# A two-layer decoder step on one core: the result sent in column groups by SP's queue, small transposes joined, decode rows of the first projection in quarters

## What is computed

```python
def block(h, p_l, pos, lw, nsa_fn, h0_re, h0_im, conv_prefix):
    z = rmsnorm(h, g_attn) @ w_in                  # queries, three pairs of K/V, branch gates, S5 input, two merge gates
    o_cmp, o_sel, o_win, rows = nsa_fn(q, kc, vc, ks, vs, kw, vw, ...)
    o = bg[..., 0:1] * o_cmp + bg[..., 1:2] * o_sel + bg[..., 2:3] * o_win
    a_out = o.reshape(B, T, Q_W) @ w_a             # mixer A
    y, hr, hi = ssm_scan(u, ...)                   # mixer B: a recurrence over the positions
    yg = gelu(y)
    b_out = (yg @ w_glu1) * sigmoid(yg @ w_glu2)
    h = h + (sigmoid(ga) * a_out + sigmoid(gb) * b_out) @ w_o
    gp, val = split(rmsnorm(h, g_ffn) @ w_up)
    ext = concatenate([conv_prefix, gp])           # two rows of state for each sequence
    conv = conv_b + sum(conv_w[j] * ext[:, j:j + T] for j in range(3))
    h = h + (gelu(conv) * val) @ w_down
    h = h + sigmoid(rmsnorm(h, g_ple) @ w_ple_gate) * (p_l @ w_ple)
    return h, rows, hr, hi, ext[:, T:]             # the last two rows of ext are an output too
```

## Time and profile before

| | us |
|---|---|
| median of 3 runs | 1161.51 (1161.04 to 1164.3) |
| profiled execution, its time | 1160.05 |
| its span, first to last instruction | 1158.2 |
| PE busy | 1113.9 |
| DVE, ACT, POOL busy | 474.6, 292.2, 157.8 |

### The profile page before, as it was taken

How to read it: one execution, slowest core, us unless ns; L and a number is a source line. 1 busy time by engine, 2 the same in 40 slices (tenths; PEclk the granted TensorE clock), 3 DMA queues, 4 the chain that set the end, 5 groups by cost and what they waited for, 6 DMA issues and landing times.

```text
span 1158.2 us, 16487 instructions
## 1 busy us (share of the span) xinstructions
PE 1113.9 (96%) x6314; PEld 918.5 (79%) x6314; DVE 474.6 (41%) x1197; ACT 292.2 (25%) x929; POOL 157.8 (14%) x276
## 2 busy tenths in 40 slices
PE   6999999999999999999999999999999999999995
PEld 4887776688888888888888878667888888888884
DVE  5889606623432222152435863472334222210031
ACT  4435424501111111210344462361112111110021
POOL 5544320003000000005003623000000000000000
PEclk9999999999999999999999999999999999999998
DMA  9653683146555553444655367222355555445431
GB/s 246 178 143 95 162 252 91 37 146 150 155 152 151 150 147 100 129 125 155 186 155 145 110 172 269 66 91 97 131 139 143 146 148 147 129 119 150 145 112 37
DMA packets 239423, 162.23 MB, mean 140 GB/s; under 512 B 25344, under 2 KB 233240, under 8 KB 239208
## 3 DMA queue, kind: packets, MB, share of 16 engines
q1 hardware_dynamic: 229858, 144.45, 43.6%
q0 software_dynamic: 4752, 14.58, 4.3%
q10 hardware_dynamic: 4736, 2.16, 0.7%
HBM read 157.94 MB, written 7.58 MB: 143 GB/s over the span
## 4 chain that ended last, share of the span: by engine, by line
PE 87%; DVE 7%; ACT 3%; issue 1%; DMA 0%; DVEq 0%; SPq 0%; POOL 0%; ACTq 0%; POOLq 0%
PE bank_act L695 40%; PE bank_dve L695 36%; DVE kT L1788 1%; PE bank_dve L997 1%; PE bank_act L880 1%; PE bank_act L1073 1%; PE bank_o L1087 1%; PE bank_o L1039 1%; ACT L1217 1%; PE bank_dve L826 1%; DVE Sf L1777 1%; DVE pcw L1795 0%; DVE vpast L1791 0%; DVE rstd L1749 0%; DVE Sf L1792 0%
## 5 line engine op out<-in xcount | busy, mean ns | idle before, releaser
L695 PE MATMUL bank_act<-xn,ring 128*128 128x264 f32 x1568 | 366.9, 391 | 6.2 <-DVE xn L1753 5.3
L695 PEld LDWEIGHTS bank_act<-xn,ring 128*128 128x128 f32 x1568 | 298.8, 192 | 64.4 <-issue 9.2
L695 PE MATMUL bank_dve<-R,ring 128*128 128x264 f32 x704 | 157.6, 386 | 0.0
L695 PE MATMUL bank_dve<-xn,ring 128*128 128x264 f32 x672 | 156.4, 386 | 0.0
L695 PEld LDWEIGHTS bank_dve<-R,ring 128*128 128x128 f32 x704 | 133.4, 190 | 22.6
L695 PEld LDWEIGHTS bank_dve<-xn,ring 128*128 128x128 f32 x672 | 127.7, 190 | 21.8
L1970 DVE TENSOR_SCALAR PT<-GX,PT 128x264 f32<-128x264 f32 x44 | 18.3, 417 | 200.6 <-ACT GX L1217 200.5
L1217 ACT ACTIVATE GX<-bank_act 128x264 f32<-128x264 f32 x44 | 17.2, 391 | 269.1 <-PE bank_act L695 269.1
L1217 ACT ACTIVATE xn<-hT 128x264 f32<-128x264 f32 x32 | 13.5, 423 | 202.4 <-DVE hT L1989 149.8
L643 POOL DMA_DIRECT2D out_dram<-kall x2 | 1.0, 520 | 454.4 <-ACT kall L1217 454.4
L1217 ACT ACTIVATE PT<-bank_act 128x10 f32<-128x10 f32 (+4 forms) x94 | 28.8, 307 | 129.7 <-PE bank_act L695 123.6
(11 more groups left out here) (372 smaller groups left out, 1371.4 us busy)
## 6 DMA issues: line engine op xcount, KB each, us to landing
ring<-in_w_up_dram SPq DMA_DIRECT2D x88, 512.0 KB, 5.1
ring<-in_w_in_dram SPq DMA_DIRECT2D x28, 1024.0 KB, 6.0
ring<-in_w_down_dram SPq DMA_DIRECT2D x32, 704.0 KB, 4.6
ring<-in_w_glu_dram SPq DMA_DIRECT2D x16, 512.0 KB, 4.5
ring<-in_w_o_dram SPq DMA_DIRECT2D x8, 1024.0 KB, 5.0
ring<-in_w_ple_gate_dram SPq DMA_DIRECT2D x8, 1024.0 KB, 5.1
PT<-in_cache_cmp_dram SPq DMA_DIRECT2D x64, 64.0 KB, 2.4
ring<-in_w_a_dram SPq DMA_DIRECT2D x8, 512.0 KB, 6.9
```

Of the source, the lines that this page charges most:

```text
L695: ins = pe.matmul(out, lhsT, rhs, start=(k == 0), stop=(k == nk - 1))
```

## The change

- The result: tiles 0 to 3 of `hT` are turned between the third and the fourth chunk of the last layer's gate product, and DVE copies them after its sixth tile. The epilogue turns tiles 4 and 5 (ACT copies), 6 and 7 (DVE copies) and the 8 decode rows (ACT copies). SP sends the prompt's rows in three DMAs of 512, 256 and 256 columns, each after the copy that it needs; ACT's queue sends the decode rows; POOL only waits.
- Compressed weights: `SP_` gets a pitch of 32, and 4 transposes of 128x128 turn all heads at once, ahead of the turn of the decode outputs; ACT copies one bank of 128x512 to `pcmp`. `head_out` reads 15 rows at partitions 0, 32, 64 or 96. So the prompt's compressed values are made on all four of these, by 8 products with 32 weight columns in place of 2 with 15 in the third bank, and ACT copies that bank in two instructions. DVE splits one product of 16 sums in two.
- Conv state: in by 4 transposes of 110x128, out by 2 of 128x110 in one bank. `conv_rows` takes 4 loads of 512-byte rows instead of 3, the output 9 DMAs instead of 2.
- Decode rows of the first projection: from a layer's second chunk on, four quarters at output rows 0, 32, 64 and 96, copied in four pieces.

```diff
+            y_rows = y_prompt.rearrange("b (t p) d -> p (b t) d", p=P)
+            for c0, c1, freed, count in ((0, 512, dve_freed, dve_jobs(DEPTH - 1, "result", 2)), (512, 768, act_freed, A_BASE[DEPTH] + 1),
+                                         (768, D, dve_freed, V_BASE[DEPTH] + 1)):
+                sp.wait_ge(freed, count)
+                sp.dma_start(y_rows[:, :, c0:c1], xrows[:, 0:2, c0:c1]).then_inc(y_out, 16)
...
+                    for s in range(NB):
+                        row = KF * ((s + 2) % 5)
+                        pool.dma_start(conv_s.rearrange("l s j (f x) -> (l s j f) x", x=P)[ds((L * NB + s) * 2 * KF + KF, KF), :],
+                                       gp_rows[row:row + KF, (s + 2) // 5, :]).then_inc(conv_out, 16)
...
-                pool.dma_start(y_prompt.rearrange("b (t p) d -> p (b t) d", p=P), xrows[:, 0:2, :]).then_inc(y_out, 16)
-                pool.dma_start(y_sample.rearrange("s a d -> s (a d)"), xrows[0:NB, 2, :]).then_inc(y_out, 16)
...
-                                for j in range(2):
-                                    last = pe.matmul(bank[64 * j:64 * j + NB, 0:n // 2], rows[k][:, SEQ:NT], w[:, k, n // 2 * j:n // 2 * (j + 1)],
+                                parts = 2 if jobs <= U_AT else 4
+                                for j in range(parts):
+                                    a, m = P // parts * j, n // parts
+                                    last = pe.matmul(bank[a:a + NB, 0:m], rows[k][:, SEQ:NT], w[:, k, m * j:m * j + m],
                                                      start=(k == 0), stop=(k == KD - 1))
...
-                    for i in range(3):
+                    for i in range(3 if j < 2 else 2):
...
+                    for i in range(4 if j == 2 else 0):
+                        for g in range(KV):
+                            c = NSEQ * KV * NCMP + (g * NSEQ + NB) * NCMP
+                            last = pe.matmul(bank[32 * i:32 * i + 32, 256 + HD * g:256 + HD * g + HD], Sf[:, c:c + 32], w2[:, 2, :],
                                              start=True, stop=True)
...
+                pe.wait_ge(c_prob, L + 1)
+                bank = act_bank()
+                for j in range(2):
+                    for t in range(2):
+                        at = 2 * P * t + P * j
+                        last = pe.transpose(bank[:, P * (2 * j + t):P * (2 * j + t + 1)], SPf[:, at:at + P], ident)
+                last.then_inc(act_ready, 1)
...
-                for f in range(KF):
-                    last = pe.transpose(bank[:, 20 * f:20 * f + 20], conv_rows[:, P * f:P * f + P], ident[0:20, 0:20])
+                for k in range(4):
+                    last = pe.transpose(bank[:, 5 * KF * k:5 * KF * (k + 1)], conv_rows[:, k, :], ident[0:5 * KF, 0:5 * KF])
...
-                for j in range(6):
-                    bank = act_bank()
-                    for f in range(4 * j, min(4 * j + 4, KF)):
-                        last = pe.transpose(bank[0:10, P * (f - 4 * j):P * (f - 4 * j) + P], gcol[:, f, :], ident)
-                    last.then_inc(act_ready, 1)
+                bank = act_bank()
+                for k in range(2):
+                    last = pe.transpose(bank[0:5 * KF, P * k:P * k + P], gcol[:, 5 * k:5 * k + 5, :].rearrange("p t f -> p (t f)"), ident)
+                last.then_inc(act_ready, 1)
...
+                    if i == 2 and L + 1 == DEPTH:
+                        pe.wait_ge(h_done, L * KD + KD + 4)
+                        for t in range(3):
+                            m = P if t < 2 else NB
+                            bank = dve_bank()
+                            for k in range(4):
+                                last = pe.transpose(bank[0:m, P * k:P * k + P], hT[:, k, P * t:P * t + m], ident)
+                            last.then_inc(dve_ready, 1)
...
-                        pieces = 1 if t < 2 else 2
+                        pieces = 1 if t < 2 else 2 if jobs <= U_AT else 4
```

More of the change, by code:

```diff
@@ L156, in probs_turned @@
 def probs_turned(L, u):
[L158 removed]
+    return act_jobs(L, "p_probs", u + 1 + sum(v <= u for v in GATES_IN_HEADS))
 def weight_chunks(L):
@@ L1446, in _ @@
                     fn(hg[:, v, :], bank[:, 0:2 * NSEQ * NCMP], ACT.Gelu_apprx_tanh, bias=pe_col[:, v:v + 1]).then_inc(act_freed, 1)
-                for j in range(3):
+                for j in range(2):
                     fn(vcmp[:, 3 * j:3 * j + 3, :], take(base)[0:NCMP, 0:3 * KVW].rearrange("p (s d) -> p s d", s=3)).then_inc(act_freed, 1)
+                bank = take(base)
+                fn(vcmp[:, 6:NB, :], bank[0:NCMP, 0:2 * KVW].rearrange("p (s d) -> p s d", s=2))
+                fn(vprompt, bank[:, 2 * KVW:3 * KVW]).then_inc(act_freed, 1)
                 act_.wait_ge(s_max, L + 1)
@@ L1529, in _ @@
                 gelu(KF - 1)
-                for j in range(6):
-                    w = P * min(4, KF - 4 * j)
-                    fn(gp_rows[:, 4 * P * j:4 * P * j + w], take(base)[0:10, 0:w]).then_inc(act_freed, 1)
+                fn(gp_rows, take(base)[0:5 * KF, 0:2 * P].rearrange("p (k x) -> p k x", k=2)).then_inc(act_freed, 1)
                 for o in range(KD):
@@ L1556, in _ @@
             n[0] = 0
-            for t in range(3):
-                m = P if t < 2 else NB
-                last = fn(xrows[0:m, t, 0:512], take(A_BASE[DEPTH])[0:m, :]).then_inc(act_freed, 1)
+            fn(xrows[:, 0:2, 512:768], take(A_BASE[DEPTH])[:].rearrange("p (t d) -> p t d", t=2)).then_inc(act_freed, 1)
+            fn(xrows[0:NB, 2, 512:D], take(A_BASE[DEPTH])[0:NB, :]).then_inc(act_freed, 1)
+            act_.wait_ge(act_freed, A_BASE[DEPTH] + 2)
+            act_.wait_ge(dve_freed, dve_jobs(DEPTH - 1, "result", 3))
+            act_.dma_start(y_sample.rearrange("s a d -> s (a d)"), xrows[0:NB, 2, :]).then_inc(y_out, 16)
         @block.vector
@@ L2010, in _ @@
                     stt(hT[:, o, :], cv[:, o % 2, :], 0.5, hT[:, o, :], MUL, ADD).then_inc(h_done, 1)
+                    if o == 5 and L + 1 == DEPTH:
+                        for t in range(3):
+                            m = P if t < 2 else NB
+                            dve.tensor_copy(xrows[0:m, t, 0:512], take(base)[0:m, :]).then_inc(dve_freed, 1)
                     if L + 1 < DEPTH:
@@ L2018, in _ @@
             n[0] = 0
-            for t in range(3):
-                m = P if t < 2 else NB
-                dve.tensor_copy(xrows[0:m, t, 512:D], take(V_BASE[DEPTH])[0:m, :]).then_inc(dve_freed, 1)
+            dve.tensor_copy(xrows[:, 0:2, 768:D], take(V_BASE[DEPTH])[:].rearrange("p (t d) -> p t d", t=2)).then_inc(dve_freed, 1)
 def constants():
```

106 lines of the change are left out of this document (52 added, 54 removed).

## The result

The changed kernel takes 1146.84 us (median of 4, 1144.20 to 1150.21); the kernel before, run again beside it, 1162.12 (1161.04 to 1164.3). The ratio is 0.9871, with a 95% interval of 0.9841 to 0.9901. The forecast was 1150, range 1143 to 1154. The profiled execution took 1144.20, its span 1142.3: 15.9 us less than the span before, where the sum of the steps had said 11.6.

What follows compares the result with a forecast made beforehand. PE was taken as the bound, busy 1113.9 of 1158.2 us. Terms -2.8 + 1.2 - 3.1 + 0 - 4.5 - 2.4 = -11.6 from the profiled 1160.05 gave 1148.45, 1150 for the median; range 1143 to 1154.

Steps and rivals of the forecast that it cites:

- E: Conv state out, between gate tiles and down product: 22 transposes per layer become 2, nothing absorbs the gain; -4.5 us.
- C: Compressed weights in the attention: 16 small transposes per layer leave, 4 wide ones hide in a wait; -3.1 us.
- D: Conv state in, ahead of the product with w_o: 22 transposes become 4, but PE only waits longer; 0.
- A: First projection's decode rows in quarters, eight blocks: 6.6 us off PE's list, mostly absorbed by waits; -2.8 us.
- B: Compressed values, third bank: a second ACT copy and more small PE products, 0.6 per layer; +1.2 us.
- F: Result at the kernel's end: earlier transposes, shorter last copies, smaller last DMA; -2.4 us.
- rival 2: Program's end: the unnamed 6.7 us after the last landing is POOL closing its queue, some 6 can go; 1144, chance 0.20.
- rival 5: Decode blocks: the four quarters run one after another at 61 ns, a block 3.9 us; 1165, chance 0.04.
- rival 4: Decode blocks: a floor on instruction spacing leaves a block at 1.7 us, gain about nothing; 1152.8, chance 0.06.
- rival 3: PE's waits for DVE or ACT absorb all the decode-quarter gain and half the compressed-weight gain; 1154, chance 0.10.
- The clock: TensorE at half clock after idle PE: a stretch costs about 1.7 us, small shifts may add or remove one; ±1.7.

Runs made afterwards that it cites:

- conv22: Changed kernel with the conv state turned out by 22 transposes per layer, six ACT copies and two DMAs as before: large products 2.24 us later at each of two places.
- turn_behind: Changed kernel with the four joined compressed-weight transposes and their ACT copy behind the turn of the decode outputs: first head 0.44 us later in each layer.
- halves: Changed kernel with all first-projection decode blocks in halves again: large products 2.04 us later over layer 0; in layer 1, 0.55 later at the first block, 1.45 earlier at the last.
- some_quarters: Changed kernel with decode quarters only in four of eight blocks, halves elsewhere: 1149.44 us in one execution; later side by side 1150.00, ratio 0.9910.
- pool_result: Changed kernel with the result's three column groups and decode rows sent by POOL's queue, not SP's and ACT's: last `hT` to POOL's last wait 4.94 us against 4.09.
- one_piece: Changed kernel with SP sending the prompt's result in one 1 MB DMA, not three: last `hT` to POOL's last wait 6.32 us against 4.09; whole kernel 1153.33.

## Why the prediction was right

**The direction and the size** came from the steps that stand on PE's path with no wait behind: E, and C with its u = 4 at nothing, were right to 0.15 us per layer. conv22 showed E alone, and turn_behind the cover that C's four wide transposes have. D at nothing was right, with the microsecond turned into a wait.

**A** was right in the main point, that the gain mostly goes into waits, and halves and some_quarters showed it block by block. One size was off: the two early blocks of layer 0 gave 1.1, not 1.6. I let both bring the third `drive` earlier and overlooked the read-out that lies between them and it, at which DVE's state is now 0.28 late; the second block gave only 0.3. The loss at layer 1's last block, +0.35, was right (0.36).

**B** was mis-sized, +0.15 for +0.6. I gave ACT's second copy the 0.2 of a copy of its own, and the smaller first copy nothing back: the pair takes 0.53 where one took 0.48. PE's eight products cost 0.44 in all, and four narrower ones left.

**F** was mis-sized by 0.8. I took 0.3 off the gain for the decode rows; but in the kernel before they landed last, and POOL's wait was over 8.62 after the last `hT`, 0.3 behind the landing that I had counted from, so that term had the wrong sign. The flight was 2.6 at most, not 2.9. Of POOL's 0.6 from DVE's last copy to its issue, pool_result puts only 0.3 on POOL itself.

**The ending** (rival 2) did not shrink: POOL's closing instruction took 5.95 us before, 5.46 after, 5.79 in pool_result. It is there without any result on POOL's queue, and half a microsecond of it is all that can be had so.

**Slower** (rival 5) and the spacing rule (rival 4) fell with the 17 ns of L890. **The waits eat it** (rival 3) fell with A's 2.2 us and C's 3.4.

**The clock** was the largest miss in the profiled execution, 2.1 us, and by luck on the right side: the range held ±1.7 for one stretch. But executions of the changed kernel differ by up to 6 us through it (1144.20 at a mean clock of 0.994, 1150.21 at 0.988), more than any part of the change. I had it as one term of the range; it is the reason why the median can be told only to some 3 us: 1146.84 the first time, 1150.21 the second, which lies on the forecast. The first lies at the low edge of the forecast's own range, 1146.5 to 1153.5; how near a median comes to 1150 depends on the stretches as much as on the sum. The prediction had named a change in their number as a sign of being wrong, and it changed, from three to two ahead of the end.

## What to carry to other kernels

On a kernel bound by one engine, cost an edit at the place where it stands: a gain counts up to the next wait that ends at another engine, and it is read there, not from the engine's total. Set traces side by side at instructions that both kernels have in the same number; the lead changes in steps, and a step of half a microsecond can be read from one execution where the times of executions differ by five. Where a half-clock stretch falls on the place in one of the two, the step is hidden; take it from two kernels that both lack the stretch. Before small waits of TensorE are left idle as harmless, look at its granted clock behind them: side by side on one chip, filling them with dead products won 5.2 us.

## What was not expected of the hardware

- The half-clock stretches move. They fall at PE's idle times (2.27 us ahead of 29, 1.50 and 1.29 at 678, 1.39 at u = 4) or behind the decode scores with their short products, last about 3.4 us and cost 1.1 to 1.8, sometimes twice the time (28 to 35, 176 to 183). The changed kernel's first profile has two, its second three, one of them of double length. Why it has more on some executions is open, as is why the same waits sometimes have none, and why filling two places brings out two others.
- At the end of the program, a transfer's flight to memory went with its size and not with its queue: 256 KB in 2.6 us on POOL's, 512 KB in 3.2, 1 MB in 4.6; on SP's 1 MB ended 4.8 after its issue, by POOL's wait. Amid the program it was another matter: in pool_result, 256 KB of `z` on POOL's queue took 13.4 us (median of six).
- POOL's closing instruction at the end lasts 5.5 to 5.9 us with or without DMAs of POOL behind the last layer: 5.46 without (the changed kernel and one_piece), 5.79 and 5.95 with.
